# Moving the score products of a sliding-attention pipeline behind the value products

## What is computed

```python
qb = q.reshape(B, NB, BLOCK, N_KV_HEADS, GROUP, HEAD_DIM)   # 4 blocks of 128 queries, 16 heads
kb, vb = band(k), band(v)                # keys of the block before and of this block
scores = einsum('bnqhgd,bnjhd->bnhgqj', qb, kb) * (HEAD_DIM ** -0.5)
scores = where(valid, scores, NEG_INF)
probs = softmax(concatenate([scores, sink], -1), -1)[..., :-1]
out = einsum('bnhgqj,bnjhd->bnqhgd', probs, vb)
...
merged = sigmoid(g_rnn) * (y_rnn @ w_br_rnn) + sigmoid(g_attn) * (y_attn @ w_br_attn)
```

## Time and profile before

| | us |
|---|---|
| device time, median of 3 runs | 2634.1 (2633.54 to 2636.47) |
| span of the profiled execution | 2633.1 |
| PE busy | 2530.3 (96%) |
| DVE busy | 1289.5 (49%) |
| ACT busy | 1095.8 (42%) |
| POOL busy | 887.7 (34%) |

### The profile page before, as it was taken

The page is one execution under the profiler, slowest core; times in us unless marked ns, Lnnn a source line. Parts: engine busy times, 40 slices in busy tenths (PEclk is TensorE's granted clock), DMA queues, the critical chain, the costliest instruction groups (busy, mean ns, idle before and its releaser), DMA issues.

```text
span 2633.1 us, 30485 instructions
## 1 busy us (share of the span) xinstructions
PE 2530.3 (96%) x12106; PEld 2040.5 (77%) x12106; DVE 1289.5 (49%) x1839; ACT 1095.8 (42%) x1716; POOL 887.7 (34%) x390
## 2 busy tenths in 40 slices
PE   8988989999899999999999999999999989999997
PEld 6767758887766888878788888766888878788886
DVE  2994468787587458353610110687367353610113
ACT  3254237666357365233322222466374243422222
POOL 4371010000331444431344344322444441344344
PEclk9998999999999999999999999999999999999999
DMA  6232349899421233331233233211333332234232
GB/s 213 89 93 61 106 148 378 337 385 341 130 72 33 88 98 99 116 111 58 73 96 120 88 96 104 73 57 49 96 96 96 113 112 65 72 96 120 88 96 80
DMA packets 220076, 318.78 MB, mean 121 GB/s; under 512 B 17184, under 2 KB 176032, under 8 KB 219808
## 3 DMA queue, kind: packets, MB, share of 16 engines
q1 hardware_dynamic: 202240, 286.34, 33.5%
q10 hardware_dynamic: 15536, 22.62, 2.6%
q0 software_dynamic: 2160, 7.89, 0.8%
HBM read 301.06 MB, written 15.75 MB: 120 GB/s over the span
## 4 chain that ended last, share of the span: by engine, by line
PE 85%; DVE 11%; ACT 2%; issue 1%; DMA 1%; DVEq 0%; POOL 0%; ACTq 0%; SPq 0%
PE ps L681 78%; PE ps L846 3%; PE ps L696 3%; DVE stats L2163 2%; DVE rows L2173 1%; DVE ix L2276 1%; DVE top L2274 1%; DVE pair_l L2453 1%; ACT pair_h L1749 1%; DVE ps L2086 0%; DVE qf L2544 0%; DMA xblk<-xs 0%; DVE vbuf L2542 0%; DVE sc L2592 0%; DVE nmax L2596 0%
## 5 line engine op out<-in xcount | busy, mean ns | idle before, releaser
L622 POOL TENSOR_TENSOR w_lo<-w_raw,w_hi 128x1024 fp32r<-128x1024 f32 x331 | 813.4, 2467 | 1391.4 <-ACT w_hi L1515 1391.3
L681 PE MATMUL ps<-x_hi,w_hi 128*128 128x512 f32 x1624 | 641.7, 395 | 9.7 <-DVE x_lo L2080 7.1
L681 PE MATMUL ps<-x_hi,w_lo 128*128 128x512 f32 x1624 | 632.7, 390 | 0.0
L681 PE MATMUL ps<-x_lo,w_hi 128*128 128x512 f32 x1624 | 632.4, 389 | 0.0
L1515 ACT ACTIVATE w_hi<-w_raw 128x1024 fp32r<-128x1024 f32 x331 | 341.4, 1054 | 501.2 <-PE ps L681 480.5
L681 PEld LDWEIGHTS ps<-x_hi,w_hi 128*128 128x128 f32 x1624 | 304.7, 188 | 92.7 <-issue 20.3
L681 PEld LDWEIGHTS ps<-x_lo,w_hi 128*128 128x128 f32 x1624 | 304.8, 188 | 64.3
L681 PEld LDWEIGHTS ps<-x_hi,w_lo 128*128 128x128 f32 x1624 | 304.9, 188 | 61.1 <-issue 0.5
L2707 DVE TENSOR_TENSOR fhd<-fsg,ps 128x512 f32<-128x512 f32 x44 | 30.1, 687 | 382.7 <-PE ps L681 382.6
L2453 DVE TENSOR_TENSOR pair_l<-pair_raw,pair_h 128x2048 fp32r<-128x2048 f32 x84 | 189.8, 2286 | 35.2 <-ACT pair_h L1749 35.1
L1749 ACT ACTIVATE pair_h<-pair_raw 128x2048 fp32r<-128x2048 f32 x84 | 157.8, 1909 | 4.4 <-ACT yb L1764 2.8
(11 more groups left out here) (410 smaller groups left out, 4295.0 us busy)
## 6 DMA issues: line engine op xcount, KB each, us to landing
w_raw<-in_w_in SPq DMA_DIRECT2D x102, 512.0 KB, 3.7
w_raw<-in_ffn_wi SPq DMA_DIRECT2D x88, 512.0 KB, 3.5
pair_raw<-in_w_gate SPq DMA_DIRECT2D x56, 512.0 KB, 6.5
pair_raw<-in_w_up SPq DMA_DIRECT2D x56, 512.0 KB, 7.9
pair_raw<-in_w_down SPq DMA_DIRECT2D x56, 512.0 KB, 7.0
w_raw<-in_ffn_wo SPq DMA_DIRECT2D x44, 512.0 KB, 3.5
w_raw<-in_w_out SPq DMA_DIRECT2D x24, 512.0 KB, 3.6
kv_raw<-in_ckv_w SPq DMA_DIRECT2D x20, 512.0 KB, 3.8
```

The costliest lines, as they stand in the source:

```text
L622: pool.tensor_tensor(w_lo[:, slot, :], w_raw[:, slot, :], w_hi[:, slot, :].bitcast(F32), ALU.subtract).then_inc(lo_done, 1)
L681: ins = pe.matmul(o, a, b, start=first, stop=last)
```

## The change

In the loop over the 32 units the scores of unit u+3 are no longer issued between the transposes of unit u and the gates' products. They are issued last in the iteration, behind the values of unit u-1. Nothing is added or removed, on PE or anywhere else.

```diff
                 for u in range(last + 1):
                     window_transposes(u)
-                    window_scores(u + 3)
                     if u in (0, 2, 4):
                         turn_query(5 + u // 2)
                     if u < last:
                         for _ in range(fill_steps(u)):
                             next(beside)
                     if u >= 1:
                         window_values(u - 1)
+                    window_scores(u + 3)
                 window_values(last)
```

## The result

| | before | after |
|---|---|---|
| device time, median of 6 runs, us | 2634.31 (2633.54 to 2636.47) | 2644.68 (2642.63 to 2646.85) |
| ratio, with its 95% interval | | 1.0032 [1.0021, 1.0042] |
| span of the profiled execution, us | 2633.1 | 2643.6 |
| sliding-attention stage, layer 1, us | 108.58 | 111.45 |
| sliding-attention stage, layer 2, us | 108.57 | 113.05 |

The changed kernel is slower by 0.32%, which is 8.4 us (5.5 to 11.1). The medians lie 10.4 us apart, a little more than that ratio gives but inside its interval. The profiled execution took 2645.54 us. It went the way of the forecast, and 2644.7 lies inside the range of 2632 to 2648, but 5.4 us above the forecast of 2639.3.

A forecast was written before the change was run, and what follows sets the result against it. PE's own order of work was taken to bound the stage, DVE not far below. New waits 9.6 less old waits 1.5 less changeovers 5.5 gave +2.6 us a layer, +5.2 for both: 2639.3 us, range 2632 to 2648.

The forecast's parts named there:

- Slots of the changeovers: PE's switches between kinds of product in the loop: 0.19 us saved in each of 29 iterations, 5.5 us a layer.
- V-S and S-T: Values followed by scores, scores followed by transposes: new pairs on PE, assumed to take 0.59 and 0.63 us.
- second rival: Not slower at all: changeover savings outweigh new waits; 2634 us, or 2628 if scores-to-transposes is cheap; chance 0.15.
- its own sign: Transposes waiting for the divisions (lines 1865, 2606) 8 to 10 us a layer; under 7 us the forecast is wrong.
- A: Iterations with one gate step: too short to cover late scores, so transposes wait; 3.9 us a layer.
- B: Two-gate-step iterations with u mod 4 = 1: transposes wait 0.16 us each, 0.8 us a layer.
- C: GpSimd's low part holding DVE's division: 0.6 us each, six times, 3.6 us a layer; a full hit 1.0.
- D: Loop's end: short iteration 29, transposes of unit 31 and values of unit 30 wait; 1.3 us a layer.
- The start-up needs no term: Iterations 3 to 7: DVE sets the pace in either order, PE only waits at transposes instead; no separate cost.
- R1: Clearly slower: longer handovers or waits feeding each other, 8.2 us more for both layers, 2647.5 us; chance 0.2.
- R3: No effect: DVE and ACT slack hides later scores and changeovers cost the same in sum; 2634 us; chance 0.1.
- R2: The second rival: not slower at all, decided by new waits below 7.0 us a layer; chance 0.15.

The follow-up runs named there:

- x4: Kernel before, with scores moved between gates and values, except in the old place where u mod 4 = 0; 2628.72 us, ratio 0.9967.
- x3: Kernel before, with scores moved to the iteration's end as in the change, but of unit u+4, not u+3; 2626.85 us, ratio 0.9964.
- x6: Changed kernel, with GpSimd's low part of the stage's eight slabs issued as two instructions of 512 columns; 2639.10 us, ratio 1.0008 against the kernel before.
- x9: Kernel before, with GpSimd's low parts of the stage's eight slabs in two instructions of half the width; 2638.31 us, ratio 1.0002.
- x1: Kernel before, with scores moved behind the values only in iterations 0 to 7, old place from 8 on; 2638.99 us, ratio 1.0007.
- x2: Kernel before, with scores moved behind the values only from iteration 8 on, old place in 0 to 7; 2641.24 us, ratio 1.0016.
- x5: Changed kernel run again with no edit, against the kernel before; 2646.33 us, ratio 1.0039.
- x8: Kernel before, with scores between gates and values for u below 9 (mostly), then unit u+4's scores at the iteration's end; 2627.28 us, ratio 0.9963.
- x7: Changed kernel, with ACT's division of unit x-1 moved ahead of its exponentials of unit x; 2639.37 us, ratio 1.0014 against the kernel before.

## Why the prediction was right in direction and low in size

**Slots of the changeovers: right.** The sum of PE's slots behind transposes, without waits, fell by 5.2 us in layer 1 and the first gate products by 0.5; 5.5 was forecast. V-S and S-T took the assumed 0.59 and 0.63, so the half of the second rival that rested on a cheap S-T falls. Transposes and gate steps pay nothing between them, and each change of form pays. This is the rule of the Trainium skill (TensorEngine Tiling, Key Properties) on changes of the tiling mode, and the trace agrees with it in the six pairs of the two orders that change form and in T-G, which doesn't. It is also why x4, with another order but three changes in most iterations, saves about as much as x3.

**The waits: right in sum, and not as they were to be read.** The forecast wanted 8 to 10 us of transposes waiting for lines 1865 and 2606, and called itself wrong below 7. In that view they have 5.4 us, and all waits in the loop 7.4, so by its own sign it failed. The sign was badly chosen, though. PE's rows overlap: a row of transposes is printed with 0.66 us and holds PE for 0.41, and up to that difference a wait leaves no gap. Counted as slots (difference of starts less the usual slot of that pair) the new waits in layer 1 are 10.6 us, some 8.4 of them without the units that wait for the rotation (4) and for the copy (22). With those that went (1.8, forecast 1.5) and 5.7 of slots this gives +3.1, against +2.87 measured. By the terms of the forecast:

| term | forecast | measured in layer 1, by slots |
|---|---|---|
| A, one-step iterations | 3.9 | 2.2 (units 10, 13, 20, 24: 0.89, 0.35, 0.46, 0.46; units 6 and 17 none) |
| B, u mod 4 = 1 | 0.8 | 0.6 (units 2 and 18, and unit 25, where u mod 4 = 0 and nothing was forecast) |
| C, GpSimd over DVE | 3.6 | 5.3 (units 3, 5, 12, 16, 22, 26: 1.84, 0.26, 0.49, 0.67, 0.91, 1.17) |
| D, the end | 1.3 | 1.2 (units 30, 31) |
| not forecast | | 1.3 (values of unit 4, behind line 2540) |
| sum | 9.6 | 10.6 |

C was forecast for divisions that a low part meets. In four places it is so: DVE's rows of line 2606 are longer ahead of units 3, 5, 12 and 22 (2.54, 1.51, 1.83 and 1.83 us). At units 16 and 26 the low part meets the copy of the sinks (2591) at the head of front(17) and front(27) instead:

```profile
813.02 2.37 POOL L622 TENSOR_TENSOR w_lo<-w_raw,w_hi 128x1024 fp32r<-128x1024 f32 x1 [7.61 <-ACT w_hi L1515]
814.33 1.08 DVE L2591 COPY sc<-sink 128x2 f32<-128x2 f32 x1 [1.18 <-PE ps L681]
...
844.32 2.37 POOL L622 TENSOR_TENSOR w_lo<-w_raw,w_hi 128x1024 fp32r<-128x1024 f32 x1 [8.46 <-ACT w_hi L1515]
845.36 1.35 DVE L2591 COPY sc<-sink 128x2 f32<-128x2 f32 x1 [1.47 <-PE ps L681]
```

The copy of two columns, 0.17 us in the earlier trace rows, takes 1.08 and 1.35 us and ends with the low part (815.4 and 846.7). All that stands behind it, the exponentials and ACT's division too, is later by as much, and PE waits 0.67 and 1.17 us. In x6 these are 0.39 and nothing. The prediction had named the copy as a thing that could be hit, but had priced only the division.

The clearest sight of A is unit 10, the first of them in a steady loop, with 0.89 where 0.85 was worked out. The second head's transposes (third row) wait for ACT:

```profile
797.44 0.49 PE L681 MATMUL ps<-ks,qf 64*128 64x128 f32 x4
797.99 0.41 PE L696 MATMUL ps<-const,sc 128*128 128x128 f32 x2
798.97 0.44 PE L696 MATMUL ps<-const,sc 128*128 128x128 f32 x2 [0.56 <-ACT sc L1865]
```

Printed as 0.56, it is 0.98 from start to start where some 0.2 is usual. Units 6 and 17, which don't wait, stand behind the waits of units 3 to 5 and of 16, which gave DVE and ACT time; x6 bears this out at units 13 and 17, for unit 6 it is my reading. So A and C are not separate terms: where a held DVE makes PE wait, the short iteration behind it costs less. That the sum came out close is in part luck, since such errors went both ways.

**"The start-up needs no term": wrong.** This is the step that failed. I held that DVE sets the pace there in either order. For the old order x9 fits that. In the new one transposes of unit 3 wait 1.84 us and values of unit 4 1.29, 3.1 together, where 1.8 of old waits went. Unit 3's wait alone is above the 1.0 that C called its full price: the division (773.53) would have ended at 773.88 without the low part, and the scores ahead of the transposes end at 774.37, so it had 0.5 us to spare and not 1.0. Forecast for iterations 0 to 7 were, by the terms, 2.2 of new waits less 1.5 of old ones and 1.5 of slots, -0.8 us a layer; x1 leaves some +0.3, beside the clock. For the iterations from 8 on the terms give +3.4, and x2 measured +2.6. The two errors, 1.1 too low and 0.8 too high, nearly cancel in the +2.6 forecast against +2.87; that part of the agreement is luck.

**The granted clock: no step at all.** The forecast took 1.00 for the whole stage. Behind the wait of unit 3 the clock fell in one layer of two, at a cost of 1.6 us, both times that the changed kernel was profiled. With 2.87 us a layer and one such stretch the change costs 7.35 us, inside the interval of 5.5 to 11.1 about the 8.4 of the runs, and at the lower end of x5's 7.1 to 13.2. Without it the cost would be 5.7, beside a forecast of 5.2. What made the medians lie 10.4 apart rather than 7.4 is not settled; it is within what the same code varies outside the stages, and how often other executions have the slow stretch is not known.

**The rivals.** R1 (clearly slower, 2647.5) had one part right, a C near its full price (5.3 of 6.0, though 1.8 of it in one place), but A and B came out lower, not higher, and most steps behind a wait had less of one or none. Its number is near by the clock, of which it says nothing. R3 falls by the waits and the slots. R2's condition, waits below 7.0 us a layer, was not met. Its idea is right in x3 and x4, which keep the gain at the changeovers and are faster than both kernels: 0.36% and 0.33% below before, x8 0.37%.

## What to carry to other kernels

Where an in-order engine alternates between kinds of work, the order of kinds and the lead of each step are two knobs: find the order with the fewest changeovers, and then move the late step one unit further ahead (x3) or past one short step (x4), so that the way through the other engines stays covered. Measure waits on PE as slots, start to start against the usual, since gaps in the view leave out what the overlap hides. And before a wait is booked at its length, look at what stands there already: a wait mended in one place came back in another, in part in x7 and in full in x9.

## What the hardware showed unexpectedly

- PE's granted clock fell to 0.52 to 0.54 for 2.5 to 3.7 us behind waits of 1.48 to 1.77 us, in a stage in which PE is otherwise busy nearly throughout. That was in 5 of 8 stages that had a wait of 1.47 us or more (the changed kernel's two profiles, x1 and x6, two layers each), and in none of the 16 stages of the other kernels, whose longest waits were up to 1.4 us. In the changed kernel one cost 1.6 us on top of the wait. What decides between the layers is open.
- A division on DVE that began 0.04 us ahead of GpSimd's low part (773.53 and 773.57) was still held to the low part's end, 2.54 us instead of 0.35. The Trainium skill (SBUF, Who interferes with whom) has the pair of ports going to the one that asks first, which by the starts of these rows would be DVE; so either that doesn't hold for these two instructions, or the printed start of a row does not tell who asked first; no run here decides it. Even a copy of two columns is held so, 1.35 us instead of 0.17 (unit 26). Cutting the low part in two took DVE's waits at transposes from 2.8 to 0.7 us (x6).
